# Depthwise taps on TensorE as 32x32 diagonal blocks

## What is computed

```python
def conformer_conv(h, w_in, b_in, dw, dw_b, ln_g, ln_b, w_out, b_out):
    d = h.shape[-1]
    a, g = jnp.split(h @ w_in + b_in, 2, axis=-1)
    u = a * jax.nn.sigmoid(g)
    u = lax.conv_general_dilated(
        u, dw[:, None, :], window_strides=(1,), padding=((30, 0),),
        dimension_numbers=('NWC', 'WIO', 'NWC'), feature_group_count=d) + dw_b
    u = jax.nn.silu(layer_norm_2(u, ln_g, ln_b))
    return u @ w_out + b_out
```

## Time and profile before

| | |
|---|---|
| median of 3 runs | 1416.16 us (1415.57 to 1416.79) |
| the profiled execution | 1417.05 us, span 1415.0 us |
| granted TensorE clock, mean | 0.982 |
| PE busy | 1346.4 us, 95% |
| DVE busy | 992.2 us, 70% |
| ACT busy | 762.1 us, 54% |
| chain that ended last | PE 78%, DVE 13%, ACT 6% |

### The profile page before, as it was taken

The page is one execution under the profiler, slowest core; times in us unless marked ns, Lnnn a source line. Parts: engine busy times, 40 slices in busy tenths (PEclk is TensorE's granted clock), DMA queues, the critical chain, the costliest instruction groups (busy, mean ns, idle before and its releaser), DMA issues.

```text
span 1415.0 us, 22752 instructions
## 1 busy us (share of the span) xinstructions
PE 1346.4 (95%) x9462; PEld 1257.8 (89%) x9462; DVE 992.2 (70%) x1538; ACT 762.1 (54%) x1057; POOL 22.5 (2%) x53
## 2 busy tenths in 40 slices
PE   6998998999989999999799996899999999999998
PEld 5997997999979999999798885888888898988887
DVE  5887977755467787778555898588876776576543
ACT  6666344436454555555265433677644687487531
POOL 0000000000000000000000000000000000000000
PEclk9999999999999999999899998999999999999999
DMA  6554553443265555544232333457776433355552
GB/s 252 189 198 179 195 219 123 179 179 134 99 243 204 204 186 210 203 179 179 90 120 100 111 117 115 152 183 300 291 271 227 157 120 120 120 184 204 180 195 71
DMA packets 34630, 247.08 MB, mean 175 GB/s; under 512 B 3872, under 2 KB 3872, under 8 KB 4960
## 3 DMA queue, kind: packets, MB, share of 16 engines
q1 hardware_dynamic: 29968, 213.38, 41.0%
q0 software_dynamic: 4560, 32.25, 6.3%
HBM read 244.57 MB, written 1.05 MB: 174 GB/s over the span
## 4 chain that ended last, share of the span: by engine, by line
PE 78%; DVE 13%; ACT 6%; issue 3%; DMA 0%; DVEq 0%; ACTq 0%
PE PS L462 14%; PE PS L404 9%; PE PS L406 9%; PE PS L405 9%; PE PS L463 7%; DVE BIG L294 5%; PE PS L483 4%; PE PS L865 3%; ACT WH L543 3%; DVE WL L556 3%; PE PS L420 2%; PE PS L422 2%; PE PS L421 2%; PE PS L742 1%; PE PS L730 1%
## 5 line engine op out<-in xcount | busy, mean ns | idle before, releaser
L556 DVE TENSOR_TENSOR WL<-RAW,WH 128x2048 fp32r<-128x2048 f32 x166 | 380.1, 2290 | 115.4 <-ACT WH L543 112.1
L543 ACT ACTIVATE WH<-RAW 128x2048 fp32r<-128x2048 f32 x166 | 317.0, 1910 | 181.4 <-PE PS L463 70.0
L404 PE MATMUL PS<-XW,WH 128*128 128x256 f32 x1024 | 300.2, 293 | 16.8 <-DVE WL L556 12.4
L406 PE MATMUL PS<-XW,WL 128*128 128x256 f32 x1024 | 292.6, 286 | 0.0
L405 PE MATMUL PS<-XW,WH 128*128 128x256 f32 x1024 | 292.6, 286 | 0.0
L404 PEld LDWEIGHTS PS<-XW,WH 128*128 128x128 f32 x1024 | 199.7, 195 | 18.3 <-DVE WL L556 12.4
L405 PEld LDWEIGHTS PS<-XW,WH 128*128 128x128 f32 x1024 | 199.5, 195 | 0.2
L406 PEld LDWEIGHTS PS<-XW,WL 128*128 128x128 f32 x1024 | 199.0, 194 | 0.0
L294 DVE SCALAR_TENSOR_TENSOR BIG<-BIG,C 128x256 f32<-128x256 f32 (+1 forms) x283 | 122.9, 498 | 35.6 <-ACT BIG L1210 19.0
L462 PE MATMUL PS<-XW,WH 128*128 128x512 f32 x392 | 141.0, 398 | 0.2
L463 PE MATMUL PS<-XW,WL 128*128 128x256 f32 x392 | 110.0, 281 | 0.0
(11 more groups left out here) (348 smaller groups left out, 2701.4 us busy)
## 6 DMA issues: line engine op xcount, KB each, us to landing
RAW<-wst SPq DMA_DIRECT2D x200, 1024.0 KB, 4.9
BIG<-wad POOLq DMA_DIRECT2D x30, 1024.0 KB, 5.1
X<-xT SPq DMA_DIRECT2D x1, 1024.0 KB, 4.9
outT<-X SPq DMA_DIRECT2D x4, 256.0 KB, 4.9
K<-cst SPq DMA_DIRECT2D x1, 640.0 KB
CB<-crow SPq DMA_DIRECT2D x1, 512.0 KB
BIG<-pT POOLq DMA_DIRECT2D x2, 256.0 KB, 4.1
C<-cols SPq DMA_DIRECT2D x1, 370.0 KB
```

What stands on the lines that cost most here:

```text
L404: pe.matmul(o, h, hl[0][:, k0 + k, :], start=(k == 0), stop=False)
L406: t = pe.matmul(o, l, hl[0][:, k0 + k, :], start=False, stop=(k == 7))
L543: ac.activation(WH[p % NS][:, :], RAW[u % NR][:, :], ACT.Copy).then_inc(S.hi.tick(p), 1)
L556: ve.tensor_tensor(WL[p % NS][:, :], RAW[u % NR][:, :], WH[p % NS][:, :].bitcast(f32), ALU.subtract).then_inc(S.lo.tick(p), 1)
```

## The change

The taps that PE does grow from nine (sixteen for the last tile) to sixteen for the tiles 0 to 4 and twenty for 5 to 7. They are no longer 128x128 diagonals: a tap is cut into four 32x32 diagonal blocks, one for each group of 32 channels. Block (r, c) of a group of four taps takes the channels 32r to 32r + 31 of U, shifted by tap q + c, and writes partitions 32c to 32c + 31 of PSUM bank 4 + r. So sixteen products of 32x32 stand for four taps, and each of the four columns c adds up every fourth tap. `pe_taps` now issues 64 products for sixteen taps, 80 for twenty.

What comes out has the columns' partial sums on different partitions. ACT copies the four banks to SBUF (`ac_partial`, 128x1024), and PE adds the columns with a stacked identity `quad` (128x32, four 32x32 identities) in four products (`pe_tap_sum`), each into its 32 partitions of bank 3. DVE adds that to CO as before, but waits on the sum.

The diagonals are written by DVE in one operation for each tile (`ve_diagonals`, 128 x 512 or 640) in place of ACT's one for each tap, two tiles' of which ACT did in the layer before. Since bank 3 to 7 are taken, the halves of the gated product now go to the banks 0, 1, 2, one half to a bank, and PE does the gate half first, then the taps of j - 1, then the value half, then the sum of the taps. SP's refill of the buffer waits on the value half, which is now the second. `FOLLOW`, `after` and the place of `after` in `ac_conv` are untouched; `ac_partial` stands where the diagonals stood, behind `after` and the bias of X.

```diff
-CST = [("ident", 128), ("ones", 128), ("neg", 128), ("gm", 896)]
+CST = [("ident", 128), ("ones", 128), ("neg", 128), ("gm", 896), ("quad", 32)]
...
+    put("quad", (j % 32 == np.arange(32)[None, :]).astype(np.float32))
...
+HALVES = {("glu", _j): ((2 * _j + 1) % 3, (2 * _j) % 3) for _j in range(2, 8)}
...
-        NP = [9] * 7 + [16]
+        NP = [16] * 5 + [20] * 3
...
-        DG = [view(10816, 9, 128), view(11968, 16, 128)]
+        DG = [view(10816 + 640 * i, 20, 32) for i in range(2)]
+        PART = [view(12096 + 1024 * i, 4, T) for i in range(2)]
...
-        def half32(pe, key, op, n, ready=None):
+        def half32(pe, key, op, n, ready=None, first=0):
 
...
-            if key in OPENED:
-                b = OPENED[key][n]
-                vacate(pe, b, key, n)
-                o = PS[b][:, 0:T + 2]
-            else:
-                b = bank_of[key]
-                if n == 0:
-                    vacate(pe, b, key)
-                o = PS[b][:, n * T:(n + 1) * T]
+            b = (OPENED if key in OPENED else HALVES)[key][n]
+            vacate(pe, b, key, n)
+            o = PS[b][:, 0:T + 2 if key in OPENED else T]
...
                 elif u - NR in direct_of_unit:
-                    sp.wait_ge(*S.mm(direct_of_unit[u - NR], 1))
+                    key = direct_of_unit[u - NR]
+                    sp.wait_ge(*S.mm(key, 1 if key in OPENED else 0))
...
-            return S.conv.ve("u", j) if ("glu", j) in OPENED else evicted(("glu", j))
+            key = ("glu", j)
+            return S.conv.ve("u", j) if key in OPENED else S.bank[HALVES[key][0]](key, 0)
 
         def pe_taps(pe, j):
-            u, b = U[j % 2], 3 + j % 2
-            pe.wait_ge(*S.conv.ac("dg", j))
+
+
+
+            u = U[j % 2]
+            pe.wait_ge(*S.conv.ve("dg", j))
             pe.wait_ge(*gated(j))
-            vacate(pe, b, "taps", j)
-            for q in range(NP[j]):
-                t = pe.matmul(PS[b][:, 0:T], DG[j % 2][:, q, :], u[:, NV[j] + q:NV[j] + q + 256], start=(q == 0), stop=(q == NP[j] - 1))
+            vacate(pe, 4, "taps", j)
+            for b in range(5, 8):
+                pe.wait_ge(S.bank[b].sem, S.bank[b].n)
+            for q in range(0, NP[j], 4):
+                for r in range(4):
+                    for c in range(4):
+                        t = pe.matmul(PS[4 + r][32 * c:32 * c + 32, 0:T], DG[j % 2][32 * r:32 * r + 32, q + c, :],
+                                      u[32 * r:32 * r + 32, NV[j] + q + c:NV[j] + q + c + 256], start=(q == 0), stop=(q + 4 == NP[j]))
             t.then_inc(S.conv.pe.tick("taps", j), 1)
+
+        def pe_tap_sum(pe, j):
+
+            pe.wait_ge(*S.bank[4]("taps", j))
+            vacate(pe, 3, "tapsum", j)
+            for r in range(4):
+                t = pe.matmul(PS[3][32 * r:32 * r + 32, 0:T], cs("quad", 0, 32), PART[j % 2][:, r, :], start=True, stop=True)
+            t.then_inc(S.conv.pe.tick("sum", j), 1)
...
             for j in range(2, 8):
-                for m in range(2):
-                    half32(pe, ("glu", j), lambda k: XC[:, k, :], m, (lambda k: pe.wait_ge(*S.ah("r0", k))) if j == 2 else None)
-                    if j == 2:
-                        pe_taps(pe, m)
-                if j > 2:
-                    pe_taps(pe, j - 1)
+                half32(pe, ("glu", j), lambda k: XC[:, k, :], 1, (lambda k: pe.wait_ge(*S.ah("r0", k))) if j == 2 else None, first=1)
+                if j == 3:
+                    pe_tap_sum(pe, 1)
+                pe_taps(pe, 0 if j == 2 else j - 1)
+                half32(pe, ("glu", j), lambda k: XC[:, k, :], 0, first=1)
+                pe_tap_sum(pe, 0 if j == 2 else j - 1)
+                if j == 2:
+                    pe_taps(pe, 1)
             pe_taps(pe, 7)
+            pe_tap_sum(pe, 7)
...
-                if i and n in (1, 2):
-                    ac.wait_ge(*S.ada(SIDE_ADA - 1))
-                    ac_diagonals(ac, n - 1)
...
-        def ac_diagonals(ac, j):
-            for q in range(NP[j]):
-                t = ac.activation(DG[j % 2][:, q, :], cs("ident"), ACT.Copy, scale=col("dw", 31 * j + NV[j] + q))
-            t.then_inc(S.conv.ac.tick("dg", j), 1)
+        def ac_partial(ac, j):
+            ac.wait_ge(*S.conv.pe("taps", j))
+            ac.activation(PART[j % 2], PSA[:, 4:8, 0:T], ACT.Copy).then_inc(S.bank[4].tick("taps", j, on="ac"), 1)
 
         def ac_conv(ac):
             for j in range(8):
@@ -1419,12 +1433,15 @@
                 else:
                     ac.wait_ge(*S.mm(key, 1))
                     ac.wait_ge(*gated(j - 2))
-                    ac.activation(SGC[j % 2], two(bank_of[key])[:, 1, :], ACT.Sigmoid, bias=col("b_in", 8 + j)).then_inc(S.conv.ac.tick("sg", j), 1)
+                    b = HALVES[key][1]
+                    ac.activation(SGC[j % 2], PS[b][:, 0:T], ACT.Sigmoid, bias=col("b_in", 8 + j)).then_inc(S.bank[b].tick(key, 1, on="ac"), 1)
                 after(ac, key)
                 ac.activation(X[:, j, :], X[:, j, :], ACT.Identity, bias=BG[:, j:j + 1]).then_inc(S.conv.ac.tick("x", j), 1)
-                if 1 <= j < 7:
-                    ac.wait_ge(*S.conv.pe("taps", j - 1))
-                    ac_diagonals(ac, j + 1)
+                if j >= 2:
+                    ac_partial(ac, 0 if j == 2 else j - 1)
+                if j == 2:
+                    ac_partial(ac, 1)
+            ac_partial(ac, 7)
...
+        def ve_diagonals(ve, j):
+
+            if j >= 2:
+                ve.wait_ge(*S.conv.pe("taps", j - 2))
+            n = NP[j]
+            ve.tensor_tensor(DG[j % 2][:, 0:n, :], bm(cs("quad", 0, 32), n), bc(col("dw", 31 * j + NV[j], n), 32), ALU.mult).then_inc(S.conv.ve.tick("dg", j), 1)
+
         def ve_taps(ve, j):
-            b = 3 + j % 2
-            ve.wait_ge(*S.conv.pe("taps", j))
+            ve.wait_ge(*S.conv.pe("sum", j))
             ve.wait_ge(*own("ve"))
-            ve.tensor_tensor(CO[:, j, :], CO[:, j, :], PS[b][:, 0:T], ALU.add).then_inc(S.bank[b].tick("taps", j, on="ve"), 1)
+            ve.tensor_tensor(CO[:, j, :], CO[:, j, :], PS[3][:, 0:T], ALU.add).then_inc(S.bank[3].tick("tapsum", j, on="ve"), 1)
...
+        def ve_glu(ve, j):
+            key, u = ("glu", j), U[j % 2]
...
+            if key in OPENED:
+                ve.wait_ge(*S.bank[OPENED[key][0]](key, 0))
+                stt(ve, u[:, 30:286], CO[:, j, :], SHC[2 * j], SGC[j], ALU.add, ALU.mult).then_inc(S.conv.ve.tick("u", j), 1)
+            else:
+                ve.wait_ge(*S.mm(key, 0))
+                b = HALVES[key][0]
+                stt(ve, u[:, 30:286], PS[b][:, 0:T], col("b_in", j), SGC[j % 2], ALU.add, ALU.mult).then_inc(S.bank[b].tick(key, 0, on="ve"), 1)
+
         def ve_conv(ve):
+            ve_diagonals(ve, 0)
             ve_glu_opened(ve, 0)
             ve_glu_opened(ve, 1)
+            ve_diagonals(ve, 1)
+            ve_glu(ve, 0)
+            ve_glu(ve, 1)
             for j in range(8):
                 key = ("glu", j)
                 u, c2 = U[j % 2], CO2[j % 2]
-                ve.wait_ge(*S.conv.ac("sg", j))
-                if j == 0:
-                    ve.wait_ge(*S.conv.gp("u"))
                 if j >= 2:
-                    ve.wait_ge(*S.conv.pe("taps", j - 2))
-                if key in OPENED:
-                    ve.wait_ge(*S.bank[OPENED[key][0]](key, 0))
-                    stt(ve, u[:, 30:286], CO[:, j, :], SHC[2 * j], SGC[j], ALU.add, ALU.mult).then_inc(S.conv.ve.tick("u", j), 1)
-                else:
-                    stt(ve, u[:, 30:286], two(bank_of[key])[:, 0, :], col("b_in", j), SGC[j % 2], ALU.add, ALU.mult).then_inc(frees(key).tick(key, on="ve"), 1)
-                ve.wait_ge(*own("ve"))
+                    ve_glu(ve, j)
+                ve.wait_ge(*gated(j))
                 ve.tensor_scalar(CO[:, j, :], u[:, 0:256], col("dw", 31 * j), col("dw_b", j), ALU.mult, ALU.add).then_inc(S.conv.ve.tick(j, 0), 1)
                 ve.tensor_scalar(c2, u[:, 1:257], col("dw", 31 * j + 1), None, ALU.mult).then_inc(S.conv.ve.tick(j, 1), 1)
                 for q in range(2, NV[j]):
@@ -2097,6 +2134,8 @@
                 ve.tensor_tensor(CO[:, j, :], CO[:, j, :], c2, ALU.add).then_inc(S.conv.ve.tick(j, "sum"), 1)
                 if j:
                     ve_taps(ve, j - 1)
+                if 1 <= j < 7:
+                    ve_diagonals(ve, j + 1)
                 if j < 7:
                     then(ve, key)
```

More of the change, by code:

```diff
@@ L463, in wide @@
             return pe.matmul(PS[b + n][:, 0:T], l, op[:, 0, :], start=False, stop=False)
-        def half32(pe, key, op, n, ready=None):
+        def half32(pe, key, op, n, ready=None, first=0):
             u = direct[key]
             w = RAW[u % NR][:, :].rearrange("p (k n) -> p k n", k=8)
-            if n == 0:
+            if n == first:
                 pe.wait_ge(*S.raw[u % NR](u))
-            if key in OPENED:
-                b = OPENED[key][n]
-                vacate(pe, b, key, n)
-                o = PS[b][:, 0:T + 2]
-            else:
```

(30 more changed lines are left out.)

## The result

| | before | after |
|---|---|---|
| median | 1415.93 us (4 runs) | 1439.85 us (4 runs, 1437.22 to 1441.54) |
| ratio, 95% interval | | 1.0166, 1.0149 to 1.0184 |
| the profiled execution | 1417.05 us, span 1415.0 | 1441.54 us, span 1439.5 |
| granted TensorE clock, mean | 0.982 | 0.971 |

The change makes the kernel 23.9 us slower: 1439.85 against the 1433 that was forecast. The page's busy line answers the earlier trace rows; alone it would not give the loss away, since PE has about the same busy time.

What follows compares the result with a forecast made beforehand. The waits before the change ran along VectorE's taps; after it, three PE stalls of 8.2 us, slower clock, taps and sums were to end the stage 16.7 us later: 1433 us, own range 1423 to 1439, full range 1423 to 1452 (0.80).

Steps and rivals of the forecast that it cites:

- short waits: PE waiting on VectorE up to the value half of tile 5, some 1.9 us.
- The taps: PE's 32x32 blocks: 0.50 us a group plus 0.3 for the switch, 2.3 for sixteen taps, 2.8 for twenty.
- rival 2: Blocks' weight loads go one after another: 0.81 us a group, 1442, or 1451 with sums in a row; chance 0.17.
- Rival 3: Blocks don't run side by side: 3.45 us a group, 14.1 for sixteen taps, 1534 in all; chance 0.04.
- The sum: PE's four products adding the columns: 0.6 us and 0.2 for the switch, 0.8.
- The halves: Each half of the gated product on PE, 3.45 us; eight of them up to tile 5's value half, 27.6.
- The value half of tile 5: On PE, it ends at 834.6 us, where before it ended at 834.05.
- Up to here nothing is won: Up to tile 5's value half, PE's sixteen taps, sum, switches and waits cost nearly what nine taps cost.
- The stall: PE idles 8.2 us before the sums of tiles 4, 5 and 6; ScalarE's copy queues behind a split awaiting its transfer.
- The clock: PE's granted clock falls after each stall's idle time, losing 2.7 us each.
- The end: Third stall, sum, slow clock, tile 7's taps, copy and sum end the stage at 895.0, 16.7 us later.
- Rival 1: PE isn't held by the copy, VectorE ends last: 13 us less than before, 1403; chance 0.13.

Runs made afterwards that it cites:

- half-width run: The changed kernel with 128 moving columns in place of 256 in every tap block: 1435.18 us, one run.
- the moved line: The changed kernel with ScalarE's copy of the tap banks ahead of the weight split for tiles 5, 6 and 7: 1415.85 us, ratio to before 0.9983.
- the run on tile 6: The changed kernel with the copy moved ahead of the weight split for tile 6 only: 1430.8 us, ratio to before 1.0091.
- the one that waits 6.12 us in the layer norm: Kernel with copies first and co 2's ScalarE split behind tile 7's copy, plus co 2's transfer held until tile 7's taps are done: 1413.63 us.
- the late load: Copies first, SP holding co 2's transfer until tile 7's taps are done: 1413.63 us; with both co 2 splits behind the layer norm, 1406.34 us.

## Why the prediction was right, and where it was off

**VectorE** is no longer the bound: no wait of PE up to tile 5 is ended by it. The 1.9 us of short waits that were laid out for it did not come.

**The taps** were taken at 0.50 a group and 0.3 for the switch; they are 0.63 and 0.18: 2.69 for sixteen (2.3 said, and 2.0 to 2.6 as the sign of blocks that overlap), 3.32 for twenty (2.8 said). That is between the forecast's value and rival 2's 0.81. The half-width run says what was mis-sized: over two streamed records a group costs 0.20, not 0.07. Rival 3 is refuted: sixteen taps take 2.69 and not 14.1. The Trainium skill's rule of program order (TensorE: Matmul & The Clock Gate, part 3, What overlaps and what doesn't) can't hold here for a block's two records against the blocks behind it, as it would give those 14.1.

**The sum** is 0.57, 0.8 said. **The halves** are 3.65 each between taps and sums, 3.45 said.

**The value half of tile 5** was to end 44.2 us after PE's first half begins; it ends 837.9 - 793.08 = 44.8 after it. The errors cancel, by luck: halves 1.5 more, taps 1.9 more, sums 0.9 less, waits 1.9 less. "Up to here nothing is won" holds.

**The stall**, forecast 8.2, is 8.02, 8.17 and 8.27, with the split 842.72 - 837.9 = 4.8 after the value half (4.86 said). Its cause is confirmed by the moved line, and the run on tile 6 shows that the three are separate.

**The clock** was to take 2.7 behind each. From the rows it took 2.6, 1.8 and 2.6: (852.82 - 847.00) - 3.65 and 0.44 in the sum for the first, and so on. The period is 868.03 - 845.99 = 22.0 and then 21.4 (21.4 said).

**The end** of the stage was to be 16.7 later; the stage is 17.9 longer.

**What was missing** is behind the stage, where the sum put nothing: 3.9 us in the profile. Of these 2.4 go up to the 28th record of the output product, with the layer norm at a granted clock of 0.53. It looks as if the clock of the stalls reached on, but kernels without stalls lose as much: from the end of the last pair sum to the end of the span the two profiles of before take 536.6 and 536.7 us, the kernels that keep stalls 539.3 to 541.1, and those without 539.4 to 540.5 (leaving out the one that waits 6.12 us in the layer norm). It comes with the change, then, but not with the stalls, and its cause stays open. With 3.9, and the 1.2 of the stage, the forecast would have been 1438.1; what is left to 1439.85 is less than two profiles of one kernel differ by ahead of the stage.

**The range.** 1439.85 lies just above the forecast's own range, 1423 to 1439, and in the part given to rival 2, whose 0.81 a group did not come: the range held it because it took in both. Its own bounds don't follow from their terms: 12.6 and 21.5 later, with 3 either way, are 1425.8 to 1440.7 on the scale of the median.

**Rival 1** said 1403 if the copy were not held. Without the stalls the stage is 9.3 shorter rather than 13; what is missing is mostly the gap of 3.46 in the taps of tile 7, which no step had. With that gap reduced the stage is 12.5 shorter. That it comes near 13 is luck: the rival has VectorE end last, and with the late load VectorE waits 1.1 to 1.2 us for PE's last sum.

## What to carry to other kernels

When an operation that nobody waited for gives its place in a queue to one that the bounding engine waits for, look at what stands ahead of it: here a split whose wait of 4.4 us had cost nothing came to hold PE for 8 us, three times, and moving one line won 24 us. Look past the end of the stage that is changed, and let a run without the stall say whether what is lost there belongs to it. And when a change multiplies the instructions of an engine, see whether its program still arrives in time beside the large transfers.

## What was not expected of the hardware

- Sixteen 32x32 fp32 products with 256 moving columns take 0.63 us, 0.43 with 128: their two records' streaming and 0.20 more, whichever of rows and columns is the inner loop.
- PE stood 3.46 to 3.74 us in the middle of its taps, waiting for no semaphore, while weight transfers ran beside them, and 0.72 when the transfer was held back; that a piece of the program comes late beside the weights is the reading that fits.
- The same kernel reached the same instruction at 790.36 and 794.26 us in two executions, at a granted clock of 0.98 and 0.97 up to 785 us.
